# Moving the constants ahead of the large tiles in on-chip memory

## The reference

```python
def first_block(x, c, ...):
    mod = silu(c) @ ada_w + ada_b              # six rows of scales and shifts
    u = rms_norm(x) * (1 + sc1) + sh1
    proj = u @ w_in                            # mLSTM + convolution on parts of it
    x = x + g1 * rms_norm(concat([h, y]) @ w_out)
    u = rms_norm(x) * (1 + sc2) + sh2
    x = x + g2 * rms_norm((silu(gt) * a) @ ffn_down)   # gt, a from u @ ffn_up
def second_block(x, ...):
    for layer in range(2):
        h = h + rmsnorm(mixer(rmsnorm(h)))             # fox_attention, hgrn2_recurrence
        h = h + rmsnorm(swiglu_ffn(rmsnorm(h)))
```

## The kernel before, in words

| tiles | first byte | modulo 64 | modulo 2048 |
|---|---|---|---|
| x; raw0; w_hi0 | 16,512; 32,896; 49,280 | 0 | 128 |
| prm (first constant) | 65,664 | 0 | 128 |
| u_hi; u_lo | 76,192; 92,576 | 32 | 416 |
| m (norm and mixer scratch) | 119,200 | 32 | 416 |
| hm, a_hi, g_hi, f_hi, ada_start (one place) | 135,584 | 32 | 416 |
| va_both; pt_hi0 (attention values, weights) | 186,784; 194,976 | 32 | 416 |
| fraw0; fraw1 (2,056 bytes each, placed as 2,080) | 119,200; 121,280 | 32; 0 | 416; 448 |

## Time and profile before

### The profile page before, as it was taken

How to read it: one execution, slowest core, us unless ns; L and a number is a source line. 1 busy time by engine, 2 the same in 40 slices (tenths; PEclk the granted TensorE clock), 3 DMA queues, 4 the chain that set the end, 5 groups by cost and what they waited for, 6 DMA issues and landing times.

```text
span 2231.9 us, 26833 instructions
## 1 busy us (share of the span) xinstructions
PE 2179.8 (98%) x9588; PEld 1707.0 (76%) x9588; DVE 1116.3 (50%) x1982; ACT 664.0 (30%) x1142; POOL 1497.8 (67%) x741
## 2 busy tenths in 40 slices
PE   7999999999999999999999999999999999999997
PEld 3877777868888887788867888886787777888885
DVE  6889984984333104777643222105877835222102
ACT  3413335122222103444442111104555534111100
POOL 5868675757777887645379777886333258777785
PEclk9999999999999999999999999999999999999999
DMA  6323223633323332222123333332222122333332
GB/s 248 101 84 95 78 83 122 250 128 103 94 91 92 99 104 85 86 76 76 48 95 95 94 94 94 99 103 81 65 67 67 58 69 82 94 94 94 94 104 85
DMA packets 56371, 215.98 MB, mean 97 GB/s; under 512 B 6216, under 2 KB 6216, under 8 KB 53088
## 3 DMA queue, kind: packets, MB, share of 16 engines
q1 hardware_dynamic: 52992, 206.96, 28.8%
q10 hardware_dynamic: 3296, 7.91, 1.0%
HBM read 212.70 MB, written 2.15 MB: 96 GB/s over the span
## 4 chain that ended last, share of the span: by engine, by line
PE 76%; DVE 11%; POOL 5%; issue 3%; ACT 2%; DMA 2%; SPq 0%; DVEq 0%; POOLq 0%; ACTq 0%
PE ps L370 60%; DVE y L2035 5%; PE ps L602 2%; POOL w_lo L979 2%; POOL w_hi L973 2%; DMA raw<-in_wstream 2%; PE ps L407 2%; PE ps L1283 1%; PE ps L393 1%; PE ps L1191 1%; PE ps L394 1%; PE ps L397 1%; DVE qk L2046 1%; PE ps L1314 1%; PE ps L1420 1%
## 5 line engine op out<-in xcount | busy, mean ns | idle before, releaser
L979 POOL TENSOR_TENSOR w_lo<-raw,w_hi 128x1024 fp32r<-128x1024 f32 x335 | 815.5, 2434 | 200.3 <-ACT w_hi L1878 176.4
L973 POOL TENSOR_TENSOR w_hi<-raw,ones 128x1024 fp32r<-128x1024 f32 x304 | 580.7, 1910 | 402.9 <-DMA raw<-in_wstream 402.4
L370 PE MATMUL ps<-u_hi,w_hi 128*128 128x512 f32 x1760 | 715.8, 407 | 6.1 <-DVE qk L2046 2.4
L370 PE MATMUL ps<-u_lo,w_hi 128*128 128x512 f32 x1760 | 695.5, 395 | 0.0
L370 PE MATMUL ps<-u_hi,w_lo 128*128 128x512 f32 x1760 | 695.1, 395 | 0.0
L370 PEld LDWEIGHTS ps<-u_hi,w_hi 128*128 128x128 f32 x1760 | 331.4, 188 | 85.9 <-issue 6.2
L370 PEld LDWEIGHTS ps<-u_hi,w_lo 128*128 128x128 f32 x1760 | 330.2, 188 | 80.5
L370 PEld LDWEIGHTS ps<-u_lo,w_hi 128*128 128x128 f32 x1760 | 331.0, 188 | 75.7 <-issue 3.6
L370 PE MATMUL ps<-f_hi,w_hi 128*128 128x512 f32 x528 | 208.6, 395 | 0.0
L370 PE MATMUL ps<-f_lo,w_hi 128*128 128x512 f32 x528 | 208.6, 395 | 0.0
L370 PE MATMUL ps<-f_hi,w_lo 128*128 128x512 f32 x528 | 208.5, 395 | 0.0
(11 more groups left out here) (366 smaller groups left out, 2905.5 us busy)
## 6 DMA issues: line engine op xcount, KB each, us to landing
raw<-in_wstream SPq DMA_DIRECT2D x342, 512.0 KB, 3.6
ada_buf<-in_ada SPq DMA_DIRECT2D x16, 1024.0 KB, 6.1
ada_start<-in_ada SPq DMA_DIRECT2D x8, 1024.0 KB, 16.8
cbc<-decay_rows ACTq DMA_DIRECT2D x7, 512.0 KB, 3.7
x<-in_xT SPq DMA_DIRECT2D x1, 2048.0 KB, 8.2
bc<-gate_rows ACTq DMA_DIRECT2D x4, 512.0 KB, 5.3
out_T<-x ACTq DMA_DIRECT2D x8, 256.0 KB, 2.2
prm<-in_params SPq DMA_DIRECT2D x1, 357.5 KB, 3.0
```

The costliest lines, as they stand in the source:

```text
L370: last = nc.tensor.matmul(out, a, b, start=(start and k == 0 and i == 0), stop=(stop and k == nk - 1 and i == 2))
L973: g.tensor_tensor(w_hi[slot][:], raw[slot][:], ones[:, 0:1].to_broadcast([P, D]), ALU.mult).then_inc(chunk_hi, 1)
L979: g.tensor_tensor(w_lo[slot][:], raw[slot][:], w_hi[slot][:].bitcast(f32), ALU.subtract).then_inc(chunk_split, 1)
```

## The change

The lines that place `x`, `raw`, `w_lo` and `w_hi` move behind the constants, and ahead of them `here[0]` is rounded up to a multiple of 64. No instruction, no size, no order of work and no semaphore is touched; only addresses in the instructions differ.

```diff
@@ -133,10 +133,6 @@
-    x = place("x", KT * T, shape=[KT, T])
-    raw = [place(f"raw{i}", D) for i in range(SLOTS)]
-    w_lo = [nc.alloc_sbuf_tensor_at(f"w_lo{i}", [P, D], f32r, offset=here[0] - (SLOTS - i) * 4 * D) for i in range(SLOTS)]
-    w_hi = [place(f"w_hi{i}", D, f32r) for i in range(SLOTS)]
     prm = place("prm", NPRM)
     mod = place("mod", 48)
...
     next_keys = place("next_keys", P, i32, [2, P // 2])
+    here[0] = (here[0] + 63) // 64 * 64
+    x = place("x", KT * T, shape=[KT, T])
+    raw = [place(f"raw{i}", D) for i in range(SLOTS)]
+    w_lo = [nc.alloc_sbuf_tensor_at(f"w_lo{i}", [P, D], f32r, offset=here[0] - (SLOTS - i) * 4 * D) for i in range(SLOTS)]
+    w_hi = [place(f"w_hi{i}", D, f32r) for i in range(SLOTS)]
     u_hi = place("u_hi", KT * T, f32r, [KT, T])
```

## The result

The changed kernel takes 2199.52 us (median of 4 runs, 2196.79 to 2202.25) where the kernel before took 2235.24 beside it (2234.72 to 2235.70): a ratio of 0.9842, with a 95% interval of 0.983 to 0.9854. That is 35.7 us or 1.6% faster. The forecast was no change, 2235.5, with 2231 to 2240 as that case's own range. The execution profiled after took 2200.18 us with a span of 2198.1; the span before was 2231.9, so the two traces have 33.8 us between them to be explained.

The account below looks back on a forecast made before the run. TensorE's pace, 233.3 ns per matmul in dense stretches, was taken as the bound. Span 2231.9 + 0 + 0 + 0 + 0, with 3.6 us around it, gave 2235.5 us; range 2100 to 2240.

Parts of the forecast that it names:

- Steps 1 to 3: ScalarE, VectorE and GpSimd, transfers, and TensorE's weight loads: each taken as 0, with plus 1 us kept for the first.
- Step 4: TensorE's float32r moving operands, from 32 to 0 modulo 64: taken as 0, between 114 us less and 33 us more.
- The excess: TensorE's float32r matmuls over one column per clock: 13 to 15 ns at smaller sizes, 20 at 512, going with the columns.
- The plain float32 row: Plain float32 matmuls on TensorE: eight in 3.60 us, read as 429 ns each, only 2 or 3 over two clocks per column.
- The attention's rows: Attention matmuls of 384 columns: 175 ns in one turn, 180 in another, a possible 5 ns from places or rounding.
- The first rival: TensorE's products: moving operands starting at 32 modulo 64 cost 17.5 ns each; 2121 us; chance 0.43, in full or part.
- The second rival: TensorE's weight loads and moving operands, at one place modulo 512, collide: 5 ns per matmul, 33 us slower, 2268; chance 0.13.

Follow-up runs that it names:

- oneplace32: The change without its rounding, so weights and operands share one place, at 32 modulo 64; 2197.86 us, 0.9837 of the kernel before.
- apart192: The change with 192 bytes left free between weights and operands, all on multiples of 64; 2237.13 us, 1.0008 of the kernel before.
- apart256: The change with 256 bytes left free between weights and operands; 2199.96 us, 0.9842 of the kernel before.
- micro1: TensorE alone, computation left out: streaks of 48 matmuls at chosen D (moving operand's place less weights' place, modulo 256); 226.6 ns at D = 0, 233.33 at 32.
- micro2: TensorE alone, computation left out: the same streaks of 48 matmuls at more values of D and other sizes; 146.67 ns for 320 columns at D = 0.
- bursts: TensorE alone, computation left out: bursts of 9, 24 and 96 matmuls; at D = 0 231.1 to 231.9, 228.8 and 227.2 ns.
- operands64: The kernel before with only the operands rounded up to 64 bytes, weights left in place (D = 64); 2211.35 us, 0.9894 of before.

## Why the prediction was wrong

**Steps 1 to 3 were right.** The other engines, the transfers and the weight loads were each costed at nothing, and their rows after repeat those of before: 1293 ns on acc and sq (1294), 22.98 us for the first transfers (22.75), 188 ns per load (188). GpSimd's two splits, 4.35 us per chunk, still fit under 24 x 226.67 ns = 5.44 us, so the gain was not taken by the next in line in the feed-forward parts.

**Step 4, the moving operand, failed.** It was taken as 0 "because it is the value of the nearest rows": weight loads of 188 ns at 0 and at 32 modulo 64, and 0.63 us on ScalarE and 0.69 on VectorE at either. Those times are as stated, but they are of other instructions and say nothing on the distance of matmuls. The start of the operands by itself made no difference to it (226.67 ns at 32 modulo 64 in oneplace32 and at 0 in the kernel after); the difference between the two places did (233.33 ns in apart192, 226.67 in apart256). None of the three rows has TensorE's pace at two values of D, so the 0 was an estimate that no row bore out. The term was worth 6.67 ns on each product in a long run: 4,440 x 6.67 ns = 29.6 us, and the chain's three long pieces became 29.5 shorter.

**The excess was misread.** The prediction took 13 to 15 ns at the smaller sizes and 20 at 512 for a share of the columns. It doesn't go with the columns: at D = 0, over the 0.4167 ns per column of micro1 and micro2, it is 13.3 ns at 256, 320, 384 and 512 columns and 16 to 17 at 448, 480 and 496. D = 32 adds nothing at 320 and 384, 1.1 ns at 480 and 496, 3.9 at 448 and 6.67 at 512. No row of before shows the 2.4 GHz and the one column per clock with which the prediction computes. The runs show their product alone, 2.4 columns per ns (one in 0.4167 ns, micro1 and micro2, at a granted clock of 0.998 and 0.996), and its 106.7, 160 and 213.3 ns hold by that. The plain float32 row was misread beside it: eight records are four matmuls, so such a matmul takes 2 x 429 ns. The attention's rows, with 384 columns in bursts of a few matmuls, were the ones to which it looked for the effect of places. They could not show it for two reasons: at 384 columns D = 32 makes no difference (173.33 ns either way), and a run that short has not settled (bursts, at 512 columns: 231.1 to 231.9 ns over 9 matmuls at D = 0, where 226.67 come later).

**The first rival** had the right direction, and a chance of 0.43, but the wrong cause and a size nearly three times too large: 17.5 ns per product and 2121 us, where 6.67 ns were measured. That 2199.5 us lies within the stated range, 2100 to 2240, is owed to this rival alone and is luck, since the start at 32 modulo 64 that it blames costs nothing (226.67 ns with both at 32). 226.67 ns stays in the best case. The 215.8 ns with which this rival computes are what the bf16 streaks of micro1 take, 215.83; the float32r streaks of 512 columns reach it at no place tried (226.67 to 236.67).

**The second rival** had the right place to look, weights and operands at one place, and the wrong sign: one place is the best case (226.67 ns), not the collision. What the prediction held against it, that its 5 ns could be rounding, stands: the rows are of 384 columns in bursts of a few matmuls, and at that size micro1 has 173.33 ns at D = 0 and at 32. Micro1 has the kernel's paces with no other engine at work, so it is between TensorE's own two operands that the effect lies: 10 us in 1512 matmuls (352.79 against 342.73) hang on where these lie to each other.

## What to carry to other kernels

Where float32r products run in long unbroken stretches, put weights and moving operands at the same place modulo 256 bytes (226.67 ns against 233.33 at D = 32 and 192), the high and the low halves alike (231.1 to 233.7 with one product of three out of place); being on multiples of 64 is neither needed (oneplace32, 226.67) nor enough (apart192, 233.33). This is shown for weights of 128 columns and streams of 512: at 320 and 384 columns D = 32 cost nothing (146.67 and 173.33 ns at both), and with weights of 32 or 96 columns D = 32 was better than 0 (226.67 against 231.67 and 230.0). Read the pace as length over count of one unbroken piece of the chain: it resolves hundredths of a nanosecond where a group's mean (391 against 395 ns) blurs it. Where a step may depend on how two buffers lie to each other, as this one did, the time of other instructions at other places doesn't settle it; vary the pair, in streaks of TensorE alone.

## What had not been expected of the hardware

- The pace of float32r products at 512 columns depends on D with a period of 256 bytes: 226.67 ns at 0, 228.88 at 64, 231 to 237 at the others tried, 236.67 at 240. It isn't symmetric: 228.88 at 64, 233.33 at 192.
- 226.67 and 233.33 ns, the commonest paces at 512 columns, are 6.67 ns apart; at 0.4167 ns per column that is the time of 16 columns, or 64 bytes per partition. Over 213.3 ns, the time of 512 columns, they are 13.3 and 20 ns, two such steps and three; other D lie between the steps (228.88 at 64), or above them (236.67 at 240).
- bf16 (215.83 ns at 512 columns) and plain float32 (422.5 ns per record of 504 columns) show no difference between D = 0 and 32.
- While the granted clock is 0.50 (window 1125.5:1128.5 of before) the excess is gone at the four D that the kernels have there: the split products of 512 columns start 426 or 427 ns apart before (D = 32) and after (D = 0), and in operands64 (64) and apart192 (192) too, which is twice the 213.3 ns of 512 columns (426.7) and nothing over. Two starts before and two after:

```profile
1126.25 0.63 PE L602 MATMUL ps<-a_hi,w_lo 128*128 128x512 f32 x1
1126.68 0.63 PE L602 MATMUL ps<-a_hi,w_hi 128*128 128x512 f32 x1
...
351.20 0.63 PE L371 MATMUL ps<-u_lo,w_hi 128*128 128x512 f32 x1
351.63 0.63 PE L371 MATMUL ps<-u_hi,w_lo 128*128 128x512 f32 x1
```

- A run settles: after a break the first matmuls at D = 0 are slower, and the mean comes down from about 231.5 ns over 9 to 227.2 over 96.

What has the period of 256 bytes, and why 13.3 ns are lost even at D = 0, no run here settles.
